# A feed-forward's output projection by seven products instead of eight, in a float32 two-block transformer kernel on one Trainium2 core

## The reference, cut to what matters

```python
D_MODEL = 1024; SEQ = 512; D_FF_2 = 4 * D_MODEL

def hybrid_layer(x, ...):
    ...
    x = x + mixed @ w_out
    u = jax.nn.relu(rmsnorm(x, norm_ffn) @ w_ff1)      # 512 x 4096 hidden values
    return x + (u * u) @ w_ff2                          # 512 x 4096 by 4096 x 1024
```

## Time and profile before

| | |
|---|---|
| three runs | 2936.71, 2930.93, 2930.23 us; median 2930.93 |
| profiled execution | span 2933.4 us from its first to its last instruction; the page gives no time of its own around the span |
| TensorE busy | 2902.8 us, 99% of the span, 16274 matmuls |
| VectorE busy | 1517.0 us, 52% |
| ScalarE busy | 1134.2 us, 39% |
| granted TensorE clock | 0.999 of full speed over the span |
| HBM read | 308.98 MB, 106 GB/s over the span |

### The profile page before, as it was taken

One profiled execution on the slowest core, in us unless ns is written; L12 is line 12 of the kernel. 1 busy time (PEld: TensorE's weight loads), 2 busy tenths in 40 slices (PEclk: granted clock), 3 DMA queues, 4 the chain that ended last, 5 costly groups with the idle time before them and its releaser, 6 DMA issues.

```text
span 2933.4 us, 38336 instructions
## 1 busy us (share of the span) xinstructions
PE 2902.8 (99%) x16274; PEld 2397.5 (82%) x16274; DVE 1517.0 (52%) x2236; ACT 1134.2 (39%) x1749; POOL 68.0 (2%) x56
## 2 busy tenths in 40 slices
PE   7999999999999999999999999999999999999999
PEld 6778887888887777888888878888888877888887
DVE  6776656645165566623335764543333764643342
ACT  5555422235233333522225466342223455442231
POOL 0000011200000000000000000000000000000000
PEclk9999999999999999999999999999999999999999
DMA  8443355633432222233223222323322222222332
GB/s 308 158 136 116 115 187 180 200 119 101 101 87 73 73 73 80 73 101 108 91 96 94 87 73 73 101 86 101 101 91 89 87 87 73 87 97 90 101 101 86
DMA packets 223642, 313.58 MB, mean 107 GB/s; under 512 B 16400, under 2 KB 123248, under 8 KB 223472
## 3 DMA queue, kind: packets, MB, share of 16 engines
q1 hardware_dynamic: 207520, 266.96, 28.7%
q0 software_dynamic: 10880, 41.95, 4.2%
q10 hardware_dynamic: 5072, 2.23, 0.3%
HBM read 308.98 MB, written 2.11 MB: 106 GB/s over the span
## 4 chain that ended last, share of the span: by engine, by line
PE 92%; DVE 3%; ACT 2%; DMA 1%; issue 1%; SPq 0%; DVEq 0%; ACTq 0%
PE G L2140 47%; PE G L2147 25%; PE G L2199 6%; PE G L2182 4%; PE X L2465 1%; DMA raw<-in_hgrn_w_in 1%; PE X L2244 1%; PE G L2165 1%; DMA ada_raw<-in_ada_w 1%; PE X L2479 1%; PE X L2565 1%; PE X L2575 1%; PE G L2521 1%; PE X L2476 1%; DVE acc L1330 0%
## 5 line engine op out<-in xcount | busy, mean ns | idle before, releaser
L2140 PE MATMUL G<-u_hi,w_hi 128*128 128x512 f32 x2096 | 835.5, 399 | 1.8 <-issue 1.8
L2140 PE MATMUL G<-u_hi,w_lo 128*128 128x512 f32 x2096 | 818.1, 390 | 0.0
L2140 PE MATMUL G<-u_lo,w_hi 128*128 128x512 f32 x2096 | 817.6, 390 | 0.0
L1291 DVE TENSOR_TENSOR w_lo<-raw,w_hi 128x2048 fp32r<-128x2048 f32 (+3 forms) x238 | 535.9, 2254 | 522.1 <-ACT w_hi L671 521.1
L671 ACT CAST w_hi<-raw 128x2048 fp32r<-128x2048 f32 (+3 forms) x242 | 455.1, 1882 | 529.7 <-DMA raw<-in_w_ff 243.5
L2140 PEld LDWEIGHTS G<-u_hi,w_hi 128*128 128x128 f32 x2096 | 394.0, 188 | 89.1 <-issue 9.2
L2140 PEld LDWEIGHTS G<-u_hi,w_lo 128*128 128x128 f32 x2096 | 393.8, 188 | 84.5
L2140 PEld LDWEIGHTS G<-u_lo,w_hi 128*128 128x128 f32 x2096 | 394.5, 188 | 78.7 <-issue 1.4
L2147 PE MATMUL G<-w_hi,ff_hi 128*128 128x512 f32 x448 | 174.3, 389 | 0.0
L2147 PE MATMUL G<-w_hi,ff_lo 128*128 128x512 f32 x448 | 174.3, 389 | 0.0
L2147 PE MATMUL G<-w_lo,ff_hi 128*128 128x512 f32 x448 | 174.3, 389 | 0.0
(11 more groups left out here) (462 smaller groups left out, 4206.5 us busy)
## 6 DMA issues: line engine op xcount, KB each, us to landing
raw<-in_w_ff SPq DMA_DIRECT2D x128, 512.0 KB, 4.5
raw<-in_ffn_w_in SPq DMA_DIRECT2D x88, 512.0 KB, 4.9
ada_raw<-in_ada_w POOLq DMA_DIRECT2D x40, 1024.0 KB, 5.9
raw<-in_w_in SPq DMA_DIRECT2D x56, 512.0 KB, 4.1
raw<-in_attn_w_in SPq DMA_DIRECT2D x96, 256.0 KB, 3.7
raw<-in_ffn_w_out SPq DMA_DIRECT2D x40, 512.0 KB, 4.7
raw<-in_hgrn_w_in SPq DMA_DIRECT2D x32, 512.0 KB, 4.6
raw<-in_attn_w_in SPq DMA_DIRECT2D x24, 512.0 KB, 4.6
```

Of the source, the lines that this page charges most:

```text
L1291: tt(w_lo[slot][:, 0:nk, 0:w], raw[slot][:, 0:nk, 0:w], w_hi[slot][:, 0:nk, 0:w].bitcast(F32), ALU.subtract).then_inc(s_lo, 1)
L2140: ins = mm(G[0:c1_ - c0, m, :], w[iw][:, k, c0:c1_], xs[ix][:, x0(b) + kk, :], start=first, stop=last, skip_group_check=True)
```

## The change

Three of four quarters of the second block's feed-forward output projection are computed by Winograd's form of Strassen's scheme. The feed-forward now runs in four parts of 1024 hidden features (`FF_PARTS`). In parts 0 to 2 the hidden values (512 tokens x 1024) are cut into token halves and feature halves, four quadrants A11, A12, A21, A22, and the weights (1024 x 1024) into B11 to B22. Instead of eight quadrant products (8 x 24 = 192 matmuls) there are seven of sums (`PRODUCTS`), 7 x 2 token tiles x 4 k-tiles x 3 passes = 168 matmuls. Part 3 keeps the plain form (`ff_out{l}3`, 2 blocks of 2 chunks). Each part's `ff_in` has 2 blocks instead of 4.

- **SyncE** loads the weight quadrants straight into `yT` and `tmp` (`quadrant_loads`, eight transfers of 512 KB per part), so the seven chunks of a stage `ff_st{l}{q}` need no `raw`.
- **ScalarE** squares the hidden tile itself (`hidden_part`), and writes the upper halves of quadrants and of their sums (`upper`), as well as of the weight quadrants and sums (`weights_upper`).
- **VectorE** forms the sums of hidden quadrants and their lower halves (`hidden_sums`), four sums of weight quadrants per part and the lower halves (`weights_lower`), and adds each product to one half of `h` (`products_added`). The first product, which belongs to all four quadrants of the result, is summed over the parts in `first_product` and added to `h` once, after part 2.
- **TensorE** runs the products in `products`; products 3, 5, 4 and 6 (counting from 0) accumulate on top of an earlier one in the same bank, once `s_add` says that this one has been added to `h`.

Several semaphores of the start-up and the rope tables are merged into others to make room for the new ones, and the tail `ff_out01` is now called `ff_out03`; these parts of the diff are left out. New functions stand whole.

```diff
 ADA_FIRST = 4
 SLOTS = 3
 GATE_AT = 32
+FF_PARTS = 4
+A11, A11_21, A12, A22, A22_21, A2_SUM, A_SUM = range(7)
+B11, B12_22, B_SUM3, B21, B11_12, B_SUM4, B22 = range(7)
+PRODUCTS = (A11, A11_21, A2_SUM, A12, A22_21, A22, A_SUM)
...
 def add(name, blocks, ktiles, evictor):
-    chunks = -(-ktiles // 4)
+    chunks = -(-ktiles // 4) if evictor else len(PRODUCTS)
...
     add(f"mo{l}", 2, KT, "dve")
-    for half in range(2):
-        add(f"ff_in{l}{half}", 4, KT, "act")
-        add(f"ff_out{l}{half}", 2, 16, "dve")
-c = t = inner = 0
+    for q in range(FF_PARTS):
+        add(f"ff_in{l}{q}", 2, KT, "act")
+        if q < FF_PARTS - 1:
+            add(f"ff_st{l}{q}", 1, KT, None)
+    add(f"ff_out{l}{FF_PARTS - 1}", 2, KT, "dve")
+c = t = inner = groups = 0
 freed = {"act": 4, "dve": 4}
 for name in order:
     g = plan[name]
+    if g["evictor"] is None:
+        g.update(c0=c, group=groups)
+        c += g["chunks"]
+        groups += 1
...
 with ExitStack() as room:
-    ff_hi, ff_lo = (sb(n, [P, 16, S], F32R, room) for n in ("ff_hi", "ff_lo"))
+    s_of_hi, s_of_lo = (sb(n, [P, 7, 4, 256], F32R, room) for n in ("hidden_sums_hi", "hidden_sums_lo"))
...
     relu_f, sq_f = (sb(n, [P, 2, S], F32, room) for n in ("relu_f", "sq_f"))
+spare = ada_raw[:, :, :, :].rearrange("p a k n -> p (a k n)")[:, 3200:3968]
+sums_f = [t.rearrange("p (i c) -> p i c", i=3) for t in (spare, sums_room[:, :])]
+relu_part = [cosT, sinT]
+first_product = masks[:, 0:4 * S].bitcast(F32).rearrange("p (t n) -> p t n", t=2)
+W11, W21, W22, W12 = (t[:, i:i + 4, :] for t in (yT, tmp) for i in (0, 4))
+quadrants = ((W11, 0, 0), (W22, 1, 1), (W12, 0, 1), (W21, 1, 0))
+weights_of = {B11: W11, B12_22: W12, B_SUM3: W11, B21: W21, B11_12: W11, B_SUM4: W21, B22: W22}
 hg_state = yT[:, 0:4, :].rearrange("p a (b c) -> p (a b) c", c=P)
...
+    eng.wait_ge(s_prod, 14 * g["group"] + 2 * s + 2)
+elif s < g["chunks"] - 1:
     eng.wait_ge(s_inner, g["inner0"] + b * (g["chunks"] - 1) + s + 1)
...
+def product_bank(s, t):
+    return (G[:, t, :], G[:, 2 + t, :], X[:, t, :], G[:, t, :], X[:, t, :], G[:, 2 + t, :], X[:, t, :])[s]
...
+def quadrant_loads(name, which):
+    l, q = int(name[-2]), int(name[-1])
+    w = a["w_ff2_2"][l].rearrange("(t p) n -> p t n", p=P)
+    for i in which:
+        dst, kh, nh = quadrants[i]
+        for j in range(2):
+            k0 = 8 * q + 4 * kh + 2 * j
+            sp.dma_start(dst[:, 2 * j:2 * j + 2, :], w[:, k0:k0 + 2, 512 * nh:512 * nh + 512]).then_inc(s_quad[i // 2], 16)
 sp.dma_start(con1[:, :], a["con1"]).then_inc(s_con1, 16)
 sp.dma_start(h, a["x"][0].rearrange("(b p) n -> p b n", p=P)).then_inc(s_x, 16)
...
+if g["evictor"] is None:
+    continue
...
+        if name in ("ff_in00", "ff_in10") and (b, s) == (1, 1):
+            sp.wait_ge(s_tile, g["t0"])
+            quadrant_loads(name, range(2))
         wait_used(sp, c - SLOTS)
         chunk(name, s, b)
+if name in ("ff_in00", "ff_in10"):
+    sp.wait_ge(s_tile, g["t0"] + 4)
+    quadrant_loads(name, range(2, 4))
+elif name.startswith("ff_in") and int(name[-1]) < FF_PARTS - 1:
+    sp.wait_ge(s_lo, plan[f"ff_st{name[-2]}{int(name[-1]) - 1}"]["c0"] + len(PRODUCTS))
+    quadrant_loads(name, range(4))
...
+def weights_upper(c, q, i):
+    wait_used(act, c - SLOTS)
+    if i in (B11, B22, B21):
+        act.wait_ge(s_quad[1 if i == B21 else 0], 64 * (q + 1))
+    else:
+        act.wait_ge(s_wsum, 4 * q + 1 + (B12_22, B_SUM3, B_SUM4, B11_12).index(i))
+    sc.copy(w_hi[c % SLOTS][:, :, :], weights_of[i]).then_inc(s_hi, 1)
...
+def hidden_part(name):
+    g = plan[name]
+    q = plan["ff_st" + name[-2:]]["group"]
+    squared = squared_before(q)
+    def upper(b, m):
+        t = 8 * q + 4 * b + m
+        if b == 0:
+            sc.copy(s_of_hi[:, A11, m, :], first_hidden[:, m, 0:256])
+            act.wait_ge(s_hsum, t + 1)
+            sc.copy(s_of_hi[:, A11_21, m, :], sums_f[m % 2][:, 0, :]).then_inc(s_fhi, 1)
+        else:
+            sc.copy(s_of_hi[:, A12:A22 + 1, m, :], second_hidden[:, m % 2, :].rearrange("p (i c) -> p i c", i=2))
+            act.wait_ge(s_hsum, t + 1)
+            sc.copy(s_of_hi[:, A22_21:A_SUM + 1, m, :], sums_f[m % 2]).then_inc(s_fhi, 1)
+    for b in range(2):
+        for s in range(g["chunks"]):
+            split(name, b, s)
+        for m in range(4):
+            t = 4 * b + m
+            hidden = first_hidden[:, m, :] if b == 0 else second_hidden[:, m % 2, :]
+            act.wait_ge(s_ff, squared + t - 1)
+            evicted(g, b, m, lambda: sc.activation(fold(relu_part[m % 2][:, :]), summed_tile(name, b, m), ACT.Relu))
+            act.wait_ge(s_free["act"], g["mine"] + 4 * b + m + 1)
+            if b == 0 and q:
+                act.wait_ge(s_fr, split_before(q))
+            elif b == 1 and m >= 2:
+                act.wait_ge(s_fr, split_before(q) + t - 1)
+            sc.activation(hidden, relu_part[m % 2][:, :], ACT.Square).then_inc(s_ff, 1)
+            if m:
+                act.wait_ge(s_ff, squared + t)
+                upper(b, m - 1)
+        act.wait_ge(s_ff, squared + 4 * b + 4)
+        upper(b, 3)
+    n.skip(s_ff, 8)
...
+def weights_lower(c, q, i):
+    if i == B12_22:
+        for j in range(2):
+            dve.wait_ge(s_quad[j], 64 * (q + 1))
+        tt(W12, W12, W22, ALU.add).then_inc(s_wsum, 1)
+        dve.wait_ge(s_wsum, 4 * q + 1)
+        dve.wait_ge(s_lo, c)
+        tt(W11, W11, W12, ALU.add).then_inc(s_wsum, 1)
+    dve.wait_ge(s_hi, c + 1)
+    tt(w_lo[c % SLOTS][:, :, :], weights_of[i], w_hi[c % SLOTS][:, :, :].bitcast(F32), ALU.subtract).then_inc(s_lo, 1)
+    if i == B21:
+        dve.wait_ge(s_lo, c + 1)
+        tt(W21, W21, W11, ALU.add).then_inc(s_wsum, 1)
+        dve.wait_ge(s_wsum, 4 * q + 3)
+        tt(W11, W11, W22, ALU.subtract).then_inc(s_wsum, 1)
+def products_added(name):
+    q, l = plan[name]["group"], int(name[-2])
+    first, second = slice(0, 512), slice(512, 1024)
+    into = (None, (2, second, ALU.subtract), (2, first, ALU.add), (0, first, ALU.add), (2, second, ALU.subtract), (2, first, ALU.add),
+            (0, second, ALU.subtract))
+    for s in range(len(PRODUCTS)):
+        split(name, 0, s)
+        for t in range(2):
+            dve.wait_ge(s_prod, 14 * q + 2 * s + t + 1)
+            if 14 * q + 2 * s + t >= 4:
+                dve.wait_ge(s_add, 14 * q + 2 * s + t - 3)
+            if s:
+                j, cols, op = into[s]
+                ins = tt(h[:, j + t, cols], h[:, j + t, cols], product_bank(s, t), op)
+            elif name[-1] == "0":
+                ins = v.tensor_copy(first_product[:, t, :], product_bank(s, t))
+            else:
+                ins = tt(first_product[:, t, :], first_product[:, t, :], product_bank(s, t), ALU.add)
+            ins.then_inc(s_add, 1)
+    if int(name[-1]) == FF_PARTS - 2:
+        dve.wait_ge(s_add, 14 * q + 14)
+        for j, cols, op in ((0, second, ALU.subtract), (2, first, ALU.add), (2, second, ALU.subtract)):
+            n.give(tt(h[:, j:j + 2, cols], h[:, j:j + 2, cols], first_product[:, :, :], op), s_dve)
+        n.own(s_dve)
+def hidden_sums(name):
+    g = plan[name]
+    q = plan["ff_st" + name[-2:]]["group"]
+    def lower(b, m):
+        dve.wait_ge(s_fhi, upper_before(q) + 4 * b + m + 1)
+        lo, hi = s_of_lo[:, :, m, :], s_of_hi[:, :, m, :].bitcast(F32)
+        if b == 0:
+            tt(lo[:, A11, :], first_hidden[:, m, 0:256], hi[:, A11, :], ALU.subtract)
+            ins = tt(lo[:, A11_21, :], sums_f[m % 2][:, 0, :], hi[:, A11_21, :], ALU.subtract)
+        else:
+            tt(lo[:, A12:A22 + 1, :], second_hidden[:, m % 2, :].rearrange("p (i c) -> p i c", i=2), hi[:, A12:A22 + 1, :], ALU.subtract)
+            ins = tt(lo[:, A22_21:A_SUM + 1, :], sums_f[m % 2], hi[:, A22_21:A_SUM + 1, :], ALU.subtract)
+        ins.then_inc(s_fr, 1)
+    for b in range(2):
+        for s in range(g["chunks"]):
+            split(name, b, s)
+        for m in range(4):
+            t = 4 * b + m
+            dve.wait_ge(s_ff, squared_before(q) + t + 1)
+            dve.wait_ge(s_fr, split_before(q) + t - 1)
+            a11, a21 = first_hidden[:, m, 0:256], first_hidden[:, m, 256:512]
+            sums = sums_f[m % 2]
+            if b == 0:
+                tt(sums[:, 0, :], a11, a21, ALU.subtract).then_inc(s_hsum, 1)
+            else:
+                a12, a22 = second_hidden[:, m % 2, 0:256], second_hidden[:, m % 2, 256:512]
+                link(tt(sums[:, 0, :], a22, a21, ALU.subtract))
+                link(stt(sums[:, 1, :], sums[:, 0, :], -1.0, a11, ALU.mult, ALU.subtract))
+                stt(sums[:, 2, :], sums[:, 1, :], -1.0, a12, ALU.mult, ALU.subtract).then_inc(s_hsum, 1)
+            if m:
+                lower(b, m - 1)
+        lower(b, 3)
+    for of in ("fr", "fhi", "ff"):
+        n.skip(of, 8)
...
+def products(name):
+    g, q = plan[name], plan[name]["group"]
+    before_ = plan["ff_in" + name[-2:]]
+    k_half = {A11: 0, A11_21: 0}
+    order_in_bank = {3: 0, 5: 1, 4: 2, 6: 4}
```

(48 more changed lines are left out.)

61 lines of the change are left out of this document (39 added, 22 removed).

## The result

The changed kernel takes 2916.31 us (median of 4 runs, 2915.55 to 2921.32), the kernel before beside it 2931.19 us (4 runs, 2930.23 to 2936.71): ratio 0.9948, 95% interval 0.9934 to 0.9962. It is faster by 14.9 us, which lies beyond the 0.2% bound and inside the predicted range, but 11 us above the predicted 2905.

What follows compares the result with a forecast made beforehand. TensorE, busy 99% of the span, was taken to bound the kernel. Saving 32.6 us and losing 6.8 at the fifth products gave -25.8 from the 2930.9 us median: 2905 us, range 2897 to 2920.

Steps and rivals of the forecast that it cites:

- TensorE's saving: Six groups take 168 matmuls instead of 192; 144 fewer at 0.2267 us each save 32.6 us.
- (a) hidden tiles: Hidden sums and lower halves at the end of `ff_in` finish at 7.7, needed after 10.88: hidden, no cost.
- (b) the fifth product: TensorE waits 1.1 us per group for VectorE's fifth weights and addition to `h`; 6.8 us in six groups.
- (c) the next `ff_in`: Its first chunk, loaded once the fifth product frees the slot, is ready in time; cost 0 to 0.3 us a group.
- (d) quadrants: Weight quadrant transfers in parts 1 and 2 land at -17, before the -12.0 limit: hidden.
- The third rival: Quadrants land like single pairs, with 5.6 us of wait in four groups, 1.5 in two: 2924 us; chance 0.04.
- the slower one: Quadrant transfers as slow as the slowest pair, 12.0 us in four groups, 3.9 in two: 2954 us; chance 0.04.
- (e) nothing else: SyncE's queue behind the quadrants and the `first_product` additions in a plain `ff_in` cost nothing.
- The first (no wait): Rival: TensorE doesn't wait at the fifth product, so the full 32.6 us is saved: 2898 us; chance 0.10.
- the fifth: Rival: each matmul's whole 389 ns counts, so 56 us go and 2882 us remain after the waits; chance 0.02.
- The second: Rival: VectorE's chain is longer by 2.8 us a group, waits 3.9 each, 23.5 us in all: 2922 us; chance 0.12.
- main forecast: TensorE waits 0.5 to 2.4 us per group at the fifth product: 2901 to 2912.5 us; chance 0.68.

Runs made afterwards that it cites:

- the best order: Changed kernel with the heads' last split behind the first block's tiles and W11 - W22 made just ahead of the fourth weights' lower half: 2902.35 us.
- The extra operation: Changed kernel plus one VectorE sum of 2048 columns per group, behind the last hidden lower half: 2931.06 us.
- The edit at that place alone: Changed kernel with the first block's last split put behind its four tiles again, in the first part of each layer: 2910.22 us.
- Two edits: Changed kernel with the heads' last split behind the tiles (2910.22 us), or W11 - W22 made right behind the second weights' lower half (2912.24 us); together 2909.66 us.
- the base: The changed kernel, unaltered, run again beside the follow-up edits: 2919.16 us, ratio 0.9953 to the kernel before.

## Why the prediction was right in sign and 11 us short

- **TensorE's saving, 32.6 us: right.** A product of 24 takes 5.44 us from start to start, and the best order made the changed part 29.4 us shorter, with 3.1 still lost in its groups. That the tail before `z1` costs nothing held too: no wait stands there. Counting 389 ns for a matmul would have promised 56 us. The Trainium skill's page "Perfetto Trace Analysis" (section "Identifying the Most-Contended Engine") says of the busy share of matmuls that it isn't a good measure of how close a kernel is to its limit, because they are pipelined. The 389 ns beside a distance of 226.7 agree with that.
- **(a) hidden tiles: right.** The last hidden lower half was to end at 7.7, and the third weights' lower half, which follows it, started at 7.6 (2038.32 - 2030.74).
- **(b) the fifth product: right.** 1.1 us forecast; 1.0 by the list of waits, 1.27 from start to start: 7.6 instead of 6.8 us. The extra operation settled that this is a chain and no load: 2.2 us more on an engine that is idle 42% of the time came through almost whole (2.1). An operation that waits for nothing again starts 0.08 us before the one ahead of it ends (2048.58, behind 2046.37 + 2.29). The rule of the Trainium skill's page "VectorE: DVE Perf Modes" (section "The DRAIN you can't avoid"), 0.6 us a group more by the prediction's estimate, is again not what the trace shows. The same section of the Trainium skill's page adds, with a pointer to "Two Vector instructions with no wait between them", that a next operation which is not held starts earlier; with that the trace agrees.
- **(c) the next `ff_in`: right.** Its first matmul follows the seventh product without a wait.
- **(d) quadrants: right in effect.** They landed by about -14.7, since 1 GB/s moves from 2016 on, against a forecast of -17 and a limit of -12. The third rival and the slower one fall with it. Its size was off: the ten transfers took some 18 us, not 15.5, and 2.7 us of slack is thinner than the forecast made it. The "some 2" on top of 389 GB/s stood in no row.
- **(e) nothing else: wrong, the step that failed.** The prediction said that plain work around the groups costs nothing more, and went through SyncE and the additions. It never went through the *first block* of the first part, where the change moves a split ahead of the relus that free the banks of the head. Two heads lose 9.3 us: 4.0 and 3.7 of stops, and 1.6 of lower clock behind one of them. The edit at that place alone gave 8.9 us back. With this term the sum is -32.6 + 7.6 + 9.3 = -15.7; the changed part shrank by 15.8.
- **The rivals.** The first (no wait) and the fifth didn't happen. The second forecast waits of 23.5 us, all in the groups; there were 16.9, more than half of them at the heads. I had listed "TensorE waits at another product" as what would prove me wrong, and looked only among the products.
- **The range: luck.** The wait per group, 1.27 us, lies inside the 0.5 to 2.4 of the main forecast, but the time of 2916.3 lies outside the 2901 to 2912.5 that were worked out from it. It is inside the range only because that was drawn out to 2920 for the second rival, a longer chain on VectorE, which didn't occur. The 9.3 us came from a place that neither the forecast nor a rival looked at.

What was missing was to read the hand-over at the *border* of the changed stage as closely as its inside.

## What to carry to other kernels

When an instruction order is written by hand, check for each moved instruction what it now stands ahead of. A conversion that waits for a transfer must not be put in front of the evictions that free banks, even if it is "only" prefetch.

Slack on a helping engine isn't additive. Two edits that made the changed part 9.0 and 6.9 us shorter alone made it 11.0 shorter together, since both drew on the same microsecond; moving one of them by one step gave another 4.8. After an edit, read the list of the engine again and find the next due time before adding the next.

To compare runs within a few microseconds, measure in each trace from a fixed row ahead of the change to the end, and then add up from start to start where the main engine lost time. The first repeated to 0.2 us for the kernel before, but differed by 2.1 for the changed one; only the second showed that 1.8 us of each gain of the changed part over the base came from a wait in untouched code.
